# Two float32r pieces in place of three bfloat16 pieces in the gather and combine matmuls of a mixture-of-experts decoder

## The reference

```python
def moe_ffn(x, router_w, router_b, w_gate, w_up, w_down, s_gate, s_up, s_down):
    scores = jax.nn.sigmoid(x @ router_w)              # 256 tokens x 64 experts
    ...                                                # 8 experts for each token, by groups
    gate = gate / jnp.sum(gate, -1, keepdims=True) * ROUTED_SCALE
    def body(y, blk):
        tok, wt, e = blk
        xb = x[tok]
        hb = jax.nn.silu(xb @ w_gate[e]) * (xb @ w_up[e])
        return y.at[tok].add((hb @ w_down[e]) * wt[:, None]), None
    ...
    shared = (jax.nn.silu(x @ s_gate) * (x @ s_up)) @ s_down
    return y + shared
```

## Time and profile before

| | |
|---|---|
| median of 3 runs | 1562.53 us (1557.3 to 1562.65) |
| profiled execution, its span | 1560.8 us |
| TensorE busy | 1444.1 us, 93% |
| TensorE weight loads | 770.0 us, 49% |
| VectorE, ScalarE, GpSimd busy | 426.5, 389.6 and 180.7 us |
| read from memory | 444.57 MB |

### The profile page before, as it was taken

The page is one execution under the profiler, slowest core; times in us unless marked ns, Lnnn a source line. Parts: engine busy times, 40 slices in busy tenths (PEclk is TensorE's granted clock), DMA queues, the critical chain, the costliest instruction groups (busy, mean ns, idle before and its releaser), DMA issues. The chain is left out here.

```text
span 1560.8 us, 23257 instructions
## 1 busy us (share of the span) xinstructions
PE 1444.1 (93%) x8991; PEld 770.0 (49%) x9053; DVE 426.5 (27%) x963; ACT 389.6 (25%) x820; POOL 180.7 (12%) x272
## 2 busy tenths in 40 slices
PE   8896968999999999999959887899999999999995
PEld 5675834544544444544426553454454444454441
DVE  2466355111111111111134335511111111111113
ACT  2353312222222122222221241222222212222222
POOL 1001000111111011111130000011111101111112
PEclk9998999999999999999979988999999999999997
DMA  8214027999999599999843511799999959999980
GB/s 321 83 62 162 1 79 293 388 384 376 382 388 370 225 376 381 385 379 379 326 149 129 223 54 68 301 392 389 371 384 378 382 221 387 371 382 385 377 325 28
DMA packets 93652, 446.27 MB, mean 286 GB/s; under 512 B 9971, under 2 KB 12454, under 8 KB 60326
## 3 DMA queue, kind: packets, MB, share of 16 engines
q1 hardware_dynamic: 93606, 445.64, 73.7%
HBM read 444.57 MB, written 1.05 MB: 286 GB/s over the span
## 5 line engine op out<-in xcount | busy, mean ns | idle before, releaser
L377 PE MATMUL psum<-w_up_ring,moe_x_selected 128*64 128x512 f32 x2048 | 450.5, 592 | 1.0 <-DVE moe_x_selected L784 1.0
L377 PEld LDWEIGHTS psum<-w_up_ring,moe_x_selected 128*64 128x64 f32 x2048 | 147.6, 137 | 291.9 <-issue 291.9
L701 POOL TENSOR_TENSOR moe_out_low<-moe_out_rest,moe_out_middle 128x512 bf16<-128x512 f32 x128 | 145.8, 1160 | 936.1 <-ACT moe_out_middle L656 936.1
L421 PE MATMUL psum<-w_down_ring,moe_hT 128*64 128x512 f32 x1024 | 233.8, 598 | 1.5 <-ACT moe_matchT L650 1.5
L387 PE MATMUL psum<-moe_match,moe_x_part 128*128 128x128 bf16 x3072 | 203.7, 226 | 2.8 <-DVE moe_match L767 2.8
L387 PEld LDWEIGHTS psum<-moe_match,moe_x_part 128*128 128x128 bf16 x3072 | 195.2, 147 | 3.9 <-issue 2.9
L812 DVE SCALAR_TENSOR_TENSOR moe_h<-moe_silu,moe_slot_gate,psum 128x256 f32<-128x256 f32 x64 | 30.7, 480 | 395.5 <-ACT moe_silu L644 395.5
L421 PEld LDWEIGHTS psum<-w_down_ring,moe_hT 128*64 128x64 f32 x1024 | 67.8, 136 | 137.7 <-issue 135.9
L827 DVE TENSOR_TENSOR moe_out_rest<-psum,moe_out_high 128x512 f32<-128x512 f32 x64 | 44.3, 692 | 285.7 <-ACT moe_out_high L652 285.7
L644 ACT ACTIVATE moe_silu<-psum 128x256 f32<-128x256 f32 x64 | 24.7, 387 | 344.2 <-PE psum L377 344.2
L413 PE MATMUL psum<-moe_out_middle,moe_matchT 128*128 128x512 bf16 x256 | 98.6, 385 | 3.3
(11 more groups left out here) (496 smaller groups left out, 1294.1 us busy)
## 6 DMA issues: line engine op xcount, KB each, us to landing
w_up_ring<-in_moe_w_gate SPq DMA_DIRECT2D x128, 1024.0 KB, 8.4
w_up_ring<-in_moe_w_up SPq DMA_DIRECT2D x128, 1024.0 KB, 10.4
w_down_ring<-in_moe_w_down SPq DMA_DIRECT2D x128, 1024.0 KB, 9.4
w_up_ring<-in_ev_w_in SPq DMA_DIRECT2D x4, 2048.0 KB, 11.4
w_up_ring<-in_od_w_in SPq DMA_DIRECT2D x4, 2048.0 KB, 10.4
w_up_ring<-in_ev_w_out SPq DMA_DIRECT2D x2, 2048.0 KB, 9.6
w_up_ring<-in_od_w_out SPq DMA_DIRECT2D x2, 2048.0 KB, 7.7
ln_gain_bias<-in_ln_g SPq DMA_DIRECT2D x4, 512.0 KB, 14.0
```

Of the source, the lines that this page charges most:

```text
L377: last = nc.tensor.matmul(k.psum[e * SLOTS:(e + 1) * SLOTS, 6, :], xsel[:, kk, e * SLOTS:(e + 1) * SLOTS], up_view(slots[e], kk), start=kk ...
L421: last = nc.tensor.matmul(k.psum[e * SLOTS:(e + 1) * SLOTS, bank, :], hT[:, j * P + e * SLOTS:j * P + (e + 1) * SLOTS], k.w_down[slots[e]] ...
L701: nc.gpsimd.tensor_tensor(low[:, cols], out_rest[:, cols], middle[:, cols], ALU.subtract).then_inc(s.split, 1)
```

## The change

x, the outputs and the match matrices are held as float32r, a 4-byte type. x and the output of the experts are each split in two pieces rather than three. One match matrix covers four experts, so the gather's moving operand has 256 columns rather than 128, and the gather is done once in two pairs, in two halves of four row blocks, each half filling PSUM banks 4 and 5. The gates of the slots are fetched with float32 matmuls with one column. The match matrix is turned once in two pairs, with float32 transposes. GpSimd no longer makes a piece. The matmuls of the first token half of the combine come ahead of the turn of `h`. The layer norm's `resid` moves to a fixed place at the top of the memory, which it shares with `x_low`.

```diff
-    part = [sb(f"x_part{i}", [P, NT, D], BF16) for i in range(3)]
-    match = [sb(f"match{i}", [P, NT, 2, SLOTS], BF16) for i in range(2)]
+    x_high = sb("x_high", [P, NT, D], F32R)
+    x_low = at_top("x_low", F32R)
+    match = sb("match", [P, NT, 4, SLOTS], F32R)
+    gate_match = match[:].bitcast(F32)
+    xsel = sb("x_selected", [P, KD, 4 * SLOTS])
...
-    def pe_gather(bank, m):
-        for c in range(4):
-            kk = 4 * (bank - 4) + c
-            for i in range(3):
-                for t in range(NT):
-                    last = nc.tensor.matmul(k.psum[:, bank, c * P:(c + 1) * P], part[i][:, t, kk:D:KD],
-                                            m[:, t, :, :].rearrange("p e s -> p (e s)"),
-                                            start=i == 0 and t == 0, stop=i == 2 and t == NT - 1)
+    def pe_gather(half, sem_a, sem_b, experts=4):
+        n = experts * SLOTS
+        for b, sem in enumerate((sem_a, sem_b)):
+            for c in range(2):
+                kk = 4 * half + 2 * b + c
+                for t in range(NT):
+                    for part in (x_high, x_low):
+                        last = nc.tensor.matmul(k.psum[:, 4 + b, c * 4 * SLOTS:c * 4 * SLOTS + n], part[:, t, kk:D:KD],
+                                                match[:, t, 0:experts, :].rearrange("p e s -> p (e s)"),
+                                                start=t == 0 and part is x_high, stop=t == NT - 1 and part is x_low)
+            last.then_inc(sem, 1)
...
     def pe_combine(par, t, halves=(0, 1), begin=False):
         for half in halves:
-            for o in (high, middle, low):
-                last = nc.tensor.matmul(k.psum[:, 2 * t + half, :], matchT[par][:, t * P:(t + 1) * P],
+            for o in (high, low):
+                last = nc.tensor.matmul(k.psum[:, 2 * t + half, :], matchT[:, par, t * P:(t + 1) * P],
...
-                pe_up(slots).then_inc(s.up, 1)
+                pe_up(slots, par).then_inc(s.up, 1)
+                if not first:
+                    pe.wait_ge(s.low_a, p)
+                    pe.wait_ge(s.low_b, p)
                 if not final:
...
+                    pe_slot_gates(1 - par, pair_gates[1 - par]).then_inc(s.slot_gates, 1)
+                    if par == 1:
+                        pe_gather(0, s.gather_a, s.gather_b)
+                if not first:
+                    pe.wait_ge(s.matchT, turn + par)
+                    pe_combine(1 - par, 0, begin=second)
+                if par == 1 and not final:
+                    pe.wait_ge(s.xsel_a, 2 * turn + 3)
+                    pe.wait_ge(s.xsel_b, 2 * turn + 3)
+                    pe_gather(1, s.gather_a, s.gather_b)
+                pe.wait_ge(s.h, p + 1)
...
+                pe_turn().then_inc(s.turned, 1)
                 if not first:
-                    pe.wait_ge(s.split, 2 * p)
-                    pe_combine(1 - par, 0, begin=second)
                     pe_combine(1 - par, 1, begin=second).then_inc(s.combined, 1)
-                pe.wait_ge(s.turned_sb, 2 * p + 2)
+                if par == 0:
+                    pe_turn_match().then_inc(s.match_turned, 1)
...
-                nc.vector.tensor_tensor(out_rest[:, BANK:], turn_ps, high[:, BANK:], ALU.subtract).then_inc(s.rest_b, 1)
+                nc.vector.tensor_tensor(low[:, BANK:], turn_ps, high[:, BANK:], ALU.subtract).then_inc(s.low_b, 1)
```

More of the change, by code:

```diff
@@ L15 @@
 BF16 = mybir.dt.bfloat16
+F32R = mybir.dt.float32r
 I32 = mybir.dt.int32
@@ L37 @@
 MAX_OVER = 32
+RESID_OFFSET = 221120
 ROUTED_SCALE = 2.5
@@ L329, in moe_layer @@
     hT = sb("hT", [P, KF * P])
[L330 to L334, removed]
+    matchT = sb("matchT", [P, 2, S], F32R)
+    high = sb("out_high", [P, D], F32R)
+    low = sb("out_low", [P, D], F32R)
     score_T = sb("score_T", [N_EXP, S])
@@ L407, in pe_turn, with pe_turn_match @@
+    def pe_turn_match(pairs=2):
+        for i in range(pairs):
+            for t in range(NT):
+                last = nc.tensor.transpose(k.psum[:, 5, i * S + t * P:i * S + (t + 1) * P],
+                                           gate_match[:, t, 2 * i:2 * i + 2, :].rearrange("p e s -> p (e s)"), k.ident[:])
         return last
@@ L560, in pair @@
+                pe.wait_ge(s.turned_sb, p + 1)
                 pe.wait_ge(dn[par], 32 * (turn + 1))
[L561 to L564, removed]
+                if par == 1 and not final:
+                    pe.wait_ge(s.xsel_a, 2 * turn + 4)
                 pe_down(slots, 0, 4).then_inc(s.down_a, 1)
@@ L689, in gates_of, with pair @@
             def gates_of(p, par):
-                nc.gpsimd.tensor_tensor(pair_gates[par][:], gate_part[:, :, bass.ds(2 * p, 2), :], ones3, ALU.mult
-                                        ).then_inc(s.pair_gates, 1)
-            def pair(p, par, last_gates=False):
-                if not last_gates:
-                    pool.wait_ge(s.slot_gates, p + 1)
-                    gates_of(p + 2, par)
-                for half in range(2):
-                    cols = slice(half * BANK, (half + 1) * BANK)
-                    pool.wait_ge(s.middle, 2 * p + half + 1)
-                    nc.gpsimd.tensor_tensor(low[:, cols], out_rest[:, cols], middle[:, cols], ALU.subtract).then_inc(s.split, 1)
-            ones3 = over(over(k.ones_bf[:, 0:3], 1, 2), 1, NT)
-            pool.wait_ge(s.gate_parts, 1)
+                nc.gpsimd.tensor_copy(pair_gates[par][:].rearrange("p t e o -> p t (e o)"),
+                                      gate[:, :, bass.ds(2 * p, 2)]).then_inc(s.pair_gates, 1)
+            def pair(p, par):
+                pool.wait_ge(s.slot_gates, p + 1)
+                gates_of(p + 2, par)
+            pool.wait_ge(s.gates, 1)
             gates_of(0, 0)
@@ L807, in _, with pair @@
             nc.vector.tensor_copy(table_i[:], table[:]).then_inc(s.table_sb, 1)
-            def pair(p, par, first=False, final=False, last_match=False):
+            def pair(p, turn, par, final=False, last_match=False):
                 dve.wait_ge(s.silu, p + 1)
```

209 lines of the change are left out of this document (98 added, 111 removed).

## The result

| | before | changed |
|---|---|---|
| median, us | 1562.59 (1557.3 to 1563.44, 4 runs) | 1607.1 (1605.02 to 1607.96, 4 runs) |
| ratio, 95% interval | | 1.0291 (1.0276 to 1.0306) |
| span of the profiled execution, us | 1560.8 | 1604.5 |

Predicted were 1466 us and a gain; the changed kernel is 141 us above that, 129 above the end of the forecast (1478) and 105 above the widest bound that it names (1502). The page of the changed kernel: its span, the chain by line, and the groups of the gather (L393) and the combine (L424).

The account below looks back on a forecast made before the run. TensorE's own work bounds the loop, with transfers close behind. Savings of 52.0 us in the loop and 1.2 at the ends per layer give 1455; 9 for transfers makes 1464, plus 1.7: 1466 us, range 1445 to 1478.

Parts of the forecast that it names:

- a 4-byte load hides under 107 ns of streaming: Gather and combine on TensorE: a 107 ns weight load of 128 columns costs no extra time beside streaming that long.
- A gather matmul with 256 columns streams 107 ns in one pass: 111 ns: Gather in the expert loop: 32 matmuls at 0.111 us, 3.55 us for two pairs, before 6.04.
- The wide gather is no gain (its loads not hidden): Rival at the gather: unhidden loads add 3.4 us in two pairs, only the ends gain, 1562 us; chance 0.03.
- Combine: Combine matmuls in the expert loop: 16 at 0.215 us, 3.44 us for two pairs, before 5.16.
- Two passes: Rival at gather and combine: a float32r column costs two passes, 113 us more in the loop, 1673 us; chance 0.06.
- four passes: Rival at gather and combine: float32r costs as much as float32, 571 us more, 2131 us; chance 0.04.
- Waits: TensorE's hand-overs in the loop: with waits, even pair 13.35 us, odd pair 16.48, together 29.83 rather than 33.08.
- Transfers: Weight loads in the loop: at 400 GB/s TensorE waits 9 us over both layers; rival that they bind, 1478 to 1502, 0.13.
- the unexplained dip: Transfer rate in the earlier trace: 250 GB/s in 1063 to 1064, a reason for assuming 400 GB/s.
- TensorE's late release of places: Weight loads in the loop: much of the missing transfer rate comes from a queue run dry, which a shorter period heals.
- Entry: Start of a layer, before the first up matmuls: split gather, copies and wider match build end 2.1 us later.
- Exit: End of a layer: last combine starts 2.2 us sooner, and clock and layer norm give 0.9 more.

Follow-up runs that it names:

- flat: Changed kernel with the two pieces of x stored by row block, so the gather's stationary values lie side by side: 1475.05 us, 0.9455 of before.
- micro: Whole computation left out; streams of 24 matmuls by stationary step, width and type: float32r with 256 columns 0.127 us contiguous, 0.240 at step 8.
- micro2: Whole computation left out; more streams of 24 matmuls: float32r with 256 columns 0.175 us at step 3; step 8 0.241 to 0.246 from 256 to 512 columns.
- no_low_both: Changed kernel with x stored by row block, without the low-piece matmuls of gather and combine: 1433.51 us, 0.919 of before.
- no_low_gather: Changed kernel with x stored by row block, without the gather of the low piece of x: 1435.11 us, 0.9202 of before.

## Why the prediction was wrong

**The step that failed** is "a 4-byte load hides under 107 ns of streaming", and from it "A gather matmul with 256 columns streams 107 ns in one pass: 111 ns". It was read from the earlier trace rows, whose stationary operands are contiguous, and used for an operand with a step of 32 bytes. Measured are 241 ns in place; 32 of them in two pairs are 7.7 us rather than 3.55. Those 4.16 us, 32 times, are 133 of the 141 us of the error; undoing the stride alone gave back 132 (flat). The trace of before had one row with such an operand, which the prediction does not use: the transposes of x at the head of a layer, from float32 values 32 bytes apart (L251, 972.69 to 976.35). It would not have warned of the price. Its records start 0.213 us apart at a granted clock of 0.50, twice the 107 ns that 128 columns of a float32 record stream at full clock, so the stream alone accounts for it. It also lies below the 0.24 us of the strided streams of micro; why these loads are not slower was not tested.

**The rival that came nearest** was "The wide gather is no gain (its loads not hidden)", with 0.03 and 1562 us. Its size was wrong, since it added 107 ns for a contiguous load; and its mechanism too. In micro2 a strided load of 0.24 us beside 512 columns costs 0.246, not their sum. Loads are hidden behind the stream, and what sticks out is only what is longer. The Trainium skill (TensorE: Matmul & The Clock Gate, Weight-path perf modes) says that the fast weight load has no gain for FP32; the trace agrees in its direction, 0.109 us a contiguous float32r matmul of 128 columns against 0.056 in bfloat16, but that rule would have left 111 ns as it was. A rule that bears on the stride stands in another page of the Trainium skill (SBUF — State Buffer, Door 1: The DMA port swizzle, note on cachelines): full bandwidth needs at least two accesses to each 16-byte line. Steps of 2 and 4 in micro, 0.120 and 0.234, agree with that; in bfloat16 one value a line costs only 0.062 for 0.056. The same note of the Trainium skill calls a stride free up to 4 values of fp32; for a stationary operand step 4 already has the full price, and the measurement decides.

**Combine.** Right: 8 matmuls at 0.23 us against 0.215 predicted, one pass. Two passes and four passes, the rivals with 1673 and 2131 us, are out: 0.231 us for 512 columns in micro. The 0.215 itself was read from the up matmuls, where it does not stand for one pass (their records have 64 stationary columns; with 128 a record of 512 columns takes 0.43, micro2). The combine matmuls of before, whose starts are 0.215 us apart (791.35, 791.57, 791.78), give the same number for the right reason.

**Waits.** Right. The even pair is 13.58 us for 13.35; the gates take 0.33 us (L402 at 1079.87, the gather at 1080.20) rather than 0.5, the combine and down 0.1 us each more than they were given. No wait was added that the sum did not have.

**Transfers.** The 9 us set aside at 400 GB/s were not needed. With the queue full the engines keep 414 to 418 GB/s (flat, no_low_both), and the unexplained dip of the earlier trace rows cost nothing measurable. The argument that the missing rate was TensorE's late release of places holds: 381 GB/s at 16.5 us a pair, 369 at 17.2, 414 at 15.2.

**Entry.** Predicted 2.1 us later, measured 8.3 in layer 0. In flat the first up starts at 257.07, 2.3 us later, so in layer 0 the term was right but for the stride. In layer 1 the stretch holds the whole mixer, and flat has 194.25 us for 193.87, 0.4 more; the changed kernel has 5.25 more. The changed kernel's table of stretches in the entry of layer 0, to be held against the last three rows of flat above:

```profile
252.00:257.00 5.00, 4.05 (x16) 3.94 (x16) 2.16 (x8) 0.59 (x1) 0.31 (x2) 0.66 0.44 164
258.00:262.00 4.00, 3.96 (x16) 3.93 (x16) 0.00 (x0) 0.59 (x1) 0.00 (x0) 0.81 0.00 0
263.00:268.00 5.00, 4.94 (x14) 1.70 (x16) 3.19 (x19) 0.00 (x0) 0.00 (x0) 0.57 0.01 3
```

The two halves of the gather take 4 us each rather than 1.9. The 8.3 us are the 2.3 of flat, twice 2.1 for the strided halves, and 1.8 that lie ahead of the gather: the match matrix is built at 252.12, in flat at 250.28. These 1.8 us come before any strided gather. The 16 matmuls of the shared expert there take 8.83 us (L508, from 242.23), in flat 7.13 (L511, from 242.08), with a granted clock of 0.50 from 243.4 to 246.8 us where flat has 1.00. So nearly all of that is the clock of this one execution.

The first up matmuls are slow as well, at 0.57 of the clock: 9.2 us for 32 records rather than 7.1. The sum had no such 2.1 us; they are why the loop's row of layer 0 has 20.65 and that of layer 1 18.65. That the strided gather brought the lower clock is not shown. Each kernel has one profiled execution. In layer 1 of the changed kernel, behind the same strided gather, the first up matmuls have the full clock (from 1025.74, 12.79 us to the next pair, as in flat), and in layer 1 of no_low_gather, with contiguous operands, they have 0.50 (from 931.91, 15.22 us to the next pair).

**Exit.** The combine of the last pair starts after 1.64 us of idle time rather than 3.67, at the full clock, and the layer norm 6.13 us after the last down matmuls began rather than 8.89: 2.8 gained, predicted 3.1. The last pair, without a gather, gave 1.8 us, and the first, without a combine, 2.0 (12.79 for 14.79, in layer 1), 3.8 together; the prediction had 3.45 for them, 3.25 as for any two pairs and 0.2 more.

**The sum with the right price.** Gather 0.117, combine 0.23: the prediction's two pairs become 29.83 + 32 x 0.006 + 16 x 0.015 = 30.26 us, and flat has 30.47; the 0.2 left over stand where one group of matmuls follows another. Without the 9 us for the transfers its 1466 becomes 1457 + 32 x 0.64 = 1477, and flat took 1475.05. That is within 2 us, in part by luck: the sum has 2.1 us for the entry of layer 1, where flat shows 0.4. The plan of the change was read rightly, but for the layout of one operand.

## What to carry to other kernels

A duration read from another line is a price only for operands that lie in memory as that line's do: before a row is used, compare the access pattern, not only shape and type. When a type is widened, each stride in bytes widens with it, so look at every `a:b:step` on an operand of the changed instruction. A row that was taken at the lower clock, as the transposes of x here, shows only that its load was no slower than its slower stream, so it does not clear such an operand for the full clock. A stream of a few dozen of the very instructions, with the very layout, settles the price ahead of the change.

## What the runs showed of the hardware

- A strided 4-byte stationary operand costs 0.22 to 0.25 us a matmul, for its own 128 columns, from a step of 16 bytes on, 0.175 at 12 bytes, and nothing at 8 beside 256 columns (0.120 for 0.117 to 0.127 contiguous). The stream of the moving operand hides beside it up to 512 columns. In bfloat16 a step of 16 bytes costs 62 ns rather than 56. An exception that is not explained: the transposes of x, with a step of 32 bytes, come 0.213 us apart at a clock of 0.50.
- Float32 pays it on each of its two records: step 8, 128 columns, 0.242 us a record for 0.112 contiguous (micro). With 512 columns a record takes 0.43 us either way (micro2).
- The granted clock fell to 0.50 in micro in the stream with 128 columns and strided float32r loads, and in the entry of layer 0 of the changed kernel. It did not fall in the float32 stream of micro with the same step (1.00 over 80.7 to 92 us), nor in the loop of the changed kernel, and it fell in the entry of layer 1 of no_low_gather with contiguous operands. So no run shows that strided loads bring the lower clock.
- One core held 418 GB/s of weight loads over 150 us, with a busy share of 1.02.
